# Weight splitting in a two-attention decoder layer: upper parts of w_out on ScalarE, five tiles split by halves later, a second landing place for three early weight tiles

## The reference, cut to what matters

```python
h = rmsnorm(x, norm_w[layer])
proj = h @ w_in[layer]
(sb_q, sb_k, sb_v, fx_q, fx_k, fx_v, f_logit, m_q, gate) = jnp.split(proj, offsets, axis=-1)
sb_out = stick_breaking_attention(...)   # a = beta_t * prod(1 - beta_j), strictly causal
fx_out = forgetting_attention(...)       # softmax(q.k/8 + cumulated log forget), causal
m_out = memory_attention(...)            # softmax over the 256 memory tokens
y = jnp.concatenate([merge_heads(sb_out), merge_heads(fx_out), merge_heads(m_out)], axis=-1)
yf = y.reshape(b, s, TOTAL_HEADS, HEAD_DIM)
yf = yf * lax.rsqrt(jnp.mean(yf * yf, axis=-1, keepdims=True) + EPS)
y = yf.reshape(b, s, MIX_WIDTH) * out_norm_w[layer] * jax.nn.silu(gate)
x = x + y @ w_out[layer]
return rmsnorm(x, final_norm_w)
```

## Time and profile before

| what | value |
|---|---|
| median of 3 runs | 865.62 us (864.74 to 867.26) |
| the profiled execution | 867.77 us, of which 866.0 us are the span of its instructions |
| PE busy | 817.5 us (94% of the span) |
| DVE busy | 588.7 us (68%) |
| ACT busy | 469.7 us (54%) |
| POOL busy | 278.9 us (32%) |
| mean granted TensorE clock | 0.982 |
| DMA | 88.95 MB, mean 103 GB/s |

### The profile page before, as it was taken

One profiled execution on the slowest core, in us unless ns is written; L12 is line 12 of the kernel. 1 busy time (PEld: TensorE's weight loads), 2 busy tenths in 40 slices (PEclk: granted clock), 3 DMA queues, 4 the chain that ended last, 5 costly groups with the idle time before them and its releaser, 6 DMA issues.

```text
span 866.0 us, 12221 instructions
## 1 busy us (share of the span) xinstructions
PE 817.5 (94%) x4244; PEld 682.5 (79%) x4244; DVE 588.7 (68%) x1207; ACT 469.7 (54%) x923; POOL 278.9 (32%) x387
## 2 busy tenths in 40 slices
PE   8997986899999999999999999999999997999996
PEld 7676764788888878888888888887887886878884
DVE  5745546556767787775788786778766676775575
ACT  5744555465576555667555566655555683542231
POOL 1133979423124522422353232244323111420000
PEclk9998998999999999999999999999999999999999
DMA  7013785310300320030213004030301297152432
GB/s 294 25 67 128 269 285 226 123 49 25 98 25 25 98 97 25 26 98 25 79 45 98 30 21 121 25 74 25 122 26 46 78 337 286 56 170 74 171 122 97
DMA packets 33373, 88.95 MB, mean 103 GB/s; under 512 B 3352, under 2 KB 11544, under 8 KB 32288
## 3 DMA queue, kind: packets, MB, share of 16 engines
q1 hardware_dynamic: 33312, 88.17, 30.3%
HBM read 57.72 MB, written 21.53 MB: 92 GB/s over the span
## 4 chain that ended last, share of the span: by engine, by line
PE 68%; DVE 11%; POOL 8%; ACT 5%; DMA 4%; issue 3%; SPq 0%; DVEq 0%; ACTq 0%; POOLq 0%
PE banks L682 12%; PE banks L684 11%; PE banks L683 11%; PE banks L723 9%; PE banks L823 7%; PE banks L843 4%; PE banks L842 4%; PE banks L810 3%; PE banks L809 3%; POOL w_parts L1212 3%; DVE work L1446 2%; DMA w_raw<-in_w_tiles 2%; PE banks L863 2%; DVE pT L1483 1%; DVE work L1449 1%
## 5 line engine op out<-in xcount | busy, mean ns | idle before, releaser
L682 PE MATMUL banks<-hT,w_parts 128*128 128x512 f32 x576 | 241.6, 419 | 10.2 <-DVE fx_heads L1374 3.7
L684 PE MATMUL banks<-hT,w_parts 128*128 128x512 f32 x576 | 227.1, 394 | 0.0
L683 PE MATMUL banks<-hT,w_parts 128*128 128x512 f32 x576 | 226.5, 393 | 0.0
L1483 DVE TENSOR_TENSOR pT<-banks,pT 128x512 fp32r<-128x512 f32 x208 | 112.0, 564 | 128.4 <-ACT pT L1031 127.3
L1031 ACT ACTIVATE pT<-banks 128x512 fp32r<-128x512 f32 x208 | 97.1, 498 | 178.8 <-PE banks L823 178.2
L1212 POOL TENSOR_TENSOR w_parts<-w_raw,w_parts 128x1024 fp32r<-128x1024 f32 x40 | 97.1, 2426 | 129.5 <-ACT w_parts L937 129.5
L682 PEld LDWEIGHTS banks<-hT,w_parts 128*128 128x128 f32 x576 | 109.1, 189 | 27.1 <-DVE fx_heads L1374 4.4
L684 PEld LDWEIGHTS banks<-hT,w_parts 128*128 128x128 f32 x576 | 108.7, 189 | 24.5
L683 PEld LDWEIGHTS banks<-hT,w_parts 128*128 128x128 f32 x576 | 109.4, 190 | 12.7
L1220 POOL TENSOR_SCALAR_AFFINE_SELECT work<-work 128x128 f32<-128x128 f32 x64 | 31.2, 487 | 205.0 <-ACT work L1011 205.0
L1446 DVE TENSOR_TENSOR_SCAN work<-work 128x639 f32<-128x639 f32 (+3 forms) x64 | 91.7, 1434 | 7.1 <-POOL work L1220 6.6
(11 more groups left out here) (209 smaller groups left out, 1416.7 us busy)
## 6 DMA issues: line engine op xcount, KB each, us to landing
w_raw<-in_w_tiles SPq DMA_DIRECT2D x40, 512.0 KB, 3.3
hT<-wo_dram SPq DMA_DIRECT2D x16, 512.0 KB, 8.2
work<-in_w_out SPq DMA_DIRECT2D x8, 512.0 KB, 5.9
wo_dram<-fx_heads SPq DMA_DIRECT2D x8, 512.0 KB, 4.5
wo_dram<-work SPq DMA_DIRECT2D x8, 512.0 KB, 5.3
fx_heads<-fx_heads SPq DMA_DIRECT2D x8, 512.0 KB, 7.3
negL<-negL_dram SPq DMA_DIRECT2D x8, 512.0 KB, 6.7
yT_dram<-silu SPq DMA_DIRECT2D x8, 512.0 KB, 5.2
```

Source lines behind the costliest of these rows:

```text
L682: pe.matmul(o, w[:, 0, k, :], hT[:, 0, k, tok], start=(k == 0), stop=False)
L683: pe.matmul(o, w[:, 0, k, :], hT[:, 1, k, tok], start=False, stop=False)
L684: mm = pe.matmul(o, w[:, 1, k, :], hT[:, 0, k, tok], start=False, stop=(k == KT - 1))
L1483: dve.tensor_tensor(pT[:, n % 3, 1, cols], banks[:, T_BANK + n % 2, cols], pT[:, n % 3, 0, cols].bitcast(F32), ALU.subtract).then_inc(t_lo, 1)
```

## The change

1. **Upper parts of w_out by ScalarE.** POOL's L1249 is gone; `w_out_hi` on ACT makes the upper part with an activation, POOL keeps the subtraction (`w_out_lo`).
2. **Five tiles early, five by halves later.** A tile has ten places in the order of phases. Tiles 0 to 4 are loaded at the start of phase 0 and split at ticks 4, 6, 8, 10 and 12. Tiles 5 to 9 are split as ten halves of 128x512 in phases 2 to 8: in each even phase one half in `f_row(0)` (load, split, store at ticks 1, 4, 6) and two in the first row of `negL` (ticks 8, 11, 13, and 15, 18, 20; the latter two lie in the `sb` phase behind it; phase 8 has only the first). Their loads and stores are issued by ACT, not by SP: three DMAs for each half.
3. **A second place for tiles 3, 5 and 7 of w_in.** They land in `work[:, 3S:4S]`, so that a tile can be loaded while the one ahead of it is still being split. The exponential of unit 4 waits for the splits of tile 7, since it writes there.
4. **Order in the opening.** The memory keys are copied ahead of the tile loads. ACT splits tile 6 ahead of the forget gate's exponential and logarithm.
5. **VT of phase 2** moves from ticks 27 and later to ticks 22 and 24.

```diff
-            tick = max(READ_TICK[q] + 1, UNITS * (p.of - 1) + (12 if p.of == 2 else 6))
+            tick = max(READ_TICK[q] + 1, UNITS * (p.of - 1) + 6)
...
+W_OUT_AT = [(0, 4), (2, 6), (3, 8), (4, 10), (5, 12)]
+def w_out_halves():
+    out = []
+    for ph in range(2, LAST, 2):
+        for place, load, split, store in ((0, 1, 4, 6), (1, 8, 11, 13), (1, 15, 18, 20)):
+            if place and ph == LAST - 1:
+                continue
+            j, c = len(W_OUT_AT) + len(out) // 2, len(out) % 2
+            out.append(Half(j, c, place, UNITS * ph + load, UNITS * ph + split, UNITS * ph + store))
+    return out
...
+        def w_place(n):
+            return 1 if n in (3, 5, 7) else 0
+        def w_raw_of(n):
+            return work[:, 3 * S:4 * S] if w_place(n) else w_raw[:, :]
...
             def load_tile(n):
-                sp.wait_ge(w_hi, n)
-                sp.wait_ge(w_lo, n)
-                sp.dma_start(w_raw[:, :], w_tiles[n, :, :]).then_inc(w_in_dma, 16)
+                before = [i for i in range(n) if w_place(i) == w_place(n)]
+                if before:
+                    sp.wait_ge(w_hi, before[-1] + 1)
+                    sp.wait_ge(w_lo, before[-1] + 1)
+                else:
+                    sp.wait_ge(xT_hi, KT)
+                sp.dma_start(w_raw_of(n), w_tiles[n, :, :]).then_inc(w_in_dma[w_place(n)], 16)
...
-                if closes_tile(p) and p.tile + 3 < N_TILES:
+                if p.what == "memK" and p.c == 1:
+                    copy_mem_keys(q)
+                if closes_tile(p) and p.tile < 4:
+                    load_tile(p.tile + 4)
+                if closes_tile(p) and 5 <= p.tile < N_TILES - 3:
                     load_tile(p.tile + 3)
...
+                    if u == 4:
+                        act.wait_ge(w_lo, 8)
...
+                if ph % 2 and ph < LAST:
+                    act.wait_ge(wo_half_out[0], 32 * halves_in(0, ph + 2))
+                elif 0 < ph < LAST - 1:
+                    act.wait_ge(wo_half_out[1], 32 * halves_in(1, ph + 1))
...
+            def w_out_hi(j):
+                raw, hi = wo_rows[j]
+                act.wait_ge(wo_in[j], 16)
+                act.activation(hi.bitcast(F32R), raw, ACT.Copy).then_inc(wo_hi, 1)
+            def store_w_out_half(i):
+                x = W_OUT_HALF[i]
+                raw, hi = wo_half_rows[x.place]
+                act.wait_ge(wo_lo, len(W_OUT_AT) + i + 1)
+                act.dma_start(wo_dram[x.j, 0, :, x.c * CW:(x.c + 1) * CW], hi).then_inc(wo_half_out[x.place], 16)
+                act.dma_start(wo_dram[x.j, 1, :, x.c * CW:(x.c + 1) * CW], raw).then_inc(wo_half_out[x.place], 16)
...
-                if PIECE[q].what == "F" and PIECE[q].c == 1:
+                if PIECE[q].what == "memV" and PIECE[q].c == 0:
                     act.wait_ge(f_abs, 1)
...
+                for n, x in enumerate(W_OUT_HALF):
+                    if i == x.load:
+                        load_w_out_half(n)
+                    if i == x.split:
+                        w_out_half_hi(n)
+                    if i == x.store:
+                        store_w_out_half(n)
...
-            def split_w_out(j):
-                raw, hi = wo_rows[W_OUT_LOAD[j][2]]
-                pool.wait_ge(wo_in[W_OUT_LOAD[j][2]], 16 * wo_turn(j))
-                pool.tensor_scalar(hi.bitcast(F32R), raw, 1.0, None, ALU.mult).then_inc(wo_hi, 1)
+            def w_out_lo(j):
+                raw, hi = wo_rows[j]
                 pool.wait_ge(wo_hi, j + 1)
                 pool.tensor_tensor(raw.bitcast(F32R), raw, hi, ALU.subtract).then_inc(wo_lo, 1)
```

More of the change, by code:

```diff
@@ L278 @@
 GATED_AT = [(4 * ph + 2 + i, UNITS * (ph + 1) + (END_GATE_AT if ph == LAST else GATE_AT)[i]) for ph in range(N_PH) for i in range(2)]
-W_OUT_LOAD = [(0, 3, 0), (0, 3, 1), (2, 5, 2), (3, 6, 3), (5, 8, 4), (6, 9, 5), (10, 13, 2), (12, 15, 4), (14, 17, 5), (16, 25, 3)]
-W_OUT_TURNS = [1, 1, 2, 2, 2, 2]
+Half = namedtuple("Half", "j c place load split store")
+W_OUT_AT = [(0, 4), (2, 6), (3, 8), (4, 10), (5, 12)]
[8 more added lines that the diff above has]
+    return out
+W_OUT_HALF = w_out_halves()
 RES_ORDER = [0, 1, 2, 3, 6, 4, 5]
@@ L356, in region_of, with w_loaded @@
             return sb_heads if PHASES[ph][0] == "sb" else fx_heads
+        def w_place(n):
+            return 1 if n in (3, 5, 7) else 0
+        def w_loaded(n):
+            return sum(1 for i in range(n + 1) if w_place(i) == w_place(n))
+        def w_raw_of(n):
+            return work[:, 3 * S:4 * S] if w_place(n) else w_raw[:, :]
         def v_raw(of, c):
@@ L386, in hybrid_layer, with halves_before, halves_in, wo_rows_of @@
         f_u, f_one, f_a, f_m = work[0:FH, S:2 * S], work[0:FH, 2 * S:3 * S], f_row(0)[0:FH, :], f_row(1)[0:FH, :]
-        wo_rows = [(silu[:, :], negL[:, 0, :]), (negL[:, 1, :], sb_heads[:, 7 * S:8 * S].bitcast(F32))]
-        wo_rows += [(raw, fx_heads[:, i * S:(i + 1) * S].bitcast(F32)) for raw, i in
-                    ((work[:, S:2 * S], 6), (work[:, 2 * S:3 * S], 7), (f_row(0), 0), (f_row(1), 1))]
-        def wo_turn(j):
-            return sum(1 for _, _, pair in W_OUT_LOAD[:j + 1] if pair == W_OUT_LOAD[j][2])
+        wo_rows = [(silu[:, :], negL[:, 0, :])] + [(raw, fx_heads[:, i * S:(i + 1) * S].bitcast(F32)) for raw, i in
+                                                   ((work[:, S:2 * S], 6), (work[:, 2 * S:3 * S], 7), (f_row(0), 0), (f_row(1), 1))]
+        wo_half_rows = [(row[:, 0:CW], row[:, CW:S]) for row in (f_row(0), negL[:, 0, :])]
+        def halves_before(i):
+            return sum(1 for x in W_OUT_HALF[:i] if x.place == W_OUT_HALF[i].place)
+        def halves_in(place, ph):
+            return sum(1 for x in W_OUT_HALF if x.place == place and x.load < UNITS * ph)
+        def wo_rows_of(j):
+            kind, it = PHASES[j]
+            t = it + {"sb": 0, "fx": NPAIR, "mm": 2 * NPAIR}[kind]
+            return slice(t * P, (t + 1) * P)
         free_slot = (N_TILES - 2) % 2
@@ L510, in piece_end @@
                     copy_keys(p.of, q)
-                if p.what == "memK" and p.c == 1:
-                    copy_mem_keys(q)
             def small_end(n):
@@ L595, in _ @@
             sp.dma_start(diag[:, 0, 0:KT * FH], w_forget).then_inc(wf_in, 16)
-            load_tile(1)
-            load_tile(2)
+            for n in range(1, 4):
+                load_tile(n)
             for q in range(len(FIRST)):
-                if q == len(FIRST) - 1:
-                    load_w_out(0)
-                    load_w_out(1)
                 piece_end(q)
@@ L605, in _ @@
             for i in range(X0):
-                for j, (load, split, _) in enumerate(W_OUT_LOAD):
+                for j, (load, split) in enumerate(W_OUT_AT):
+                    if i == load:
+                        load_w_out(j)
                     if i == split + 2:
                         store_w_out(j)
-                    if i == load and j > 1:
-                        load_w_out(j)
                 for q in DONE[i]:
@@ L1174, in _ @@
                     split_next(len(FIRST) - 1)
+                for j, (_, split) in enumerate(W_OUT_AT):
+                    if i == split:
+                        w_out_hi(j)
+                for n, x in enumerate(W_OUT_HALF):
[5 more added lines that the diff above has]
+                        store_w_out_half(n)
                 if i in SPREAD_AT:
@@ L1300, in _ @@
                         split_lo(PIECE[q].tile + 2)
-                for j, (_, split, _) in enumerate(W_OUT_LOAD):
+                for j, (_, split) in enumerate(W_OUT_AT):
                     if i == split:
-                        split_w_out(j)
+                        w_out_lo(j)
+                for n, x in enumerate(W_OUT_HALF):
+                    if i == x.split:
+                        w_out_half_lo(n)
         @block.vector
```

81 lines of the change are left out of this document (48 added, 33 removed).

## The result

The changed kernel takes a median of 855.0 us (853.48 to 858.0, 4 runs) where the one before takes 866.44 us (864.74 to 868.18, 4 runs): ratio 0.9872, 95% interval [0.9838, 0.9907]. In a second series on one chip it took 854.64 us (852.55 to 856.52, 4 runs) against 866.54 us (9 runs): ratio 0.9861 [0.9839, 0.9883]. The forecast was 850.1 us, its range 842 to 861: the direction and most of the gain are right, 4.9 us of the size are missing. The profiled execution took 854.92 us (span 853.2), against 852.3 forecast for it and 867.77 us before.

The account below looks back on a forecast made before the run. PE bounds phases 2 to 8; earlier, one tile buffer and POOL's w_out splits make PE idle. Gains of 19.1 less 3.6 give net 15.5 us: 867.77 to 852.3, less 2.15, a median of 850.1 us, range 842 to 861.

Parts of the forecast that it names:

- Opening, 7.4 us: Start of the kernel: with two places for tiles, PE's first filling piece starts 7.4 us sooner than at 78.57.
- The gap of 2.62 and its stretch: Phase 0: fewer POOL splits ahead of tile 8's lower part let tile 9 land in time, 4.3 us gained.
- The gap of 2.17 and its stretch: Tick 19: with POOL's list empty, two small DVE operations take 0.17 us each instead of 1.97 and more, 3.7 us gained.
- The gaps of 1.07 and 4.44: Phases 0 to 2: 2.1 of 5.5 us gained; about 3.4 us stay at tick 25, behind POOL's Newton chain.
- The gap of 1.62: Tick 22: VT no longer waits for the last store out of fx_heads, 1.6 us gained.
- Added at tick 4 and at 6 to 12: ACT waits for w_out's first tile at tick 4, 1.6 us lost; four more copies at ticks 6 to 12, 1.0 lost.
- Added in phases 2 to 8: ACT's ten copies and 30 DMA issues, and POOL's ten subtractions, cost 1.0 us in all.
- rival (d): Slower: stores issued by ACT take up to 2.13 us each, half of 42.6 us reaches PE, about 871 us; chance 0.05.
- The own range: Whole kernel: the forecast's own range for the median, from the small ends of its terms, 845 to 856 us.
- (a): Phases 0 to 2: everything comes back, copies find data landed and tick 25's gap closes, 841.4 us; chance 0.12.
- (b): Late phases: each of POOL's ten subtractions holds DVE, and DVE holds PE, 12.9 us instead of 1.0, 862.0; chance 0.14.
- (c): Phases 0 and 1: POOL was not the limit, ACT holds the same gaps, only the opening counts, 861.8 us; chance 0.07.

Follow-up runs that it names:

- experiment 5: The kernel before with only the second place for w_in tiles and the new opening order, w_out all on POOL: 858.88 us, ratio to before 0.9898.
- experiment 6: The changed kernel with POOL making the upper parts of w_out again, halves and new places kept: 851.95 us, ratio to before 0.9818.
- experiment 7: The changed kernel with two extra POOL subtractions of 128x1024 started at tick 19: 856.17 us, ratio to before 0.9876.
- experiment 8: The changed kernel with one extra POOL subtraction of 128x2048 started at tick 19: 856.06 us, ratio to before 0.9876.
- experiment 1: The changed kernel measured again with no edit: 854.64 us, ratio to before 0.9861.
- experiment 10: The changed kernel with half stores by SP, early splits later, phase 1's spread two ticks later, and upper parts by POOL: 844.91 us, ratio to before 0.9739.

## Why the prediction was right, and where its sizes were off

*Opening, 7.4 us: right.* The trace has 7.97, of which 0.78 is a difference that was there at PE's first weights matmul (18.18 before, 17.40 after), so 7.2. The last split ahead of it ends at 70.45, as the sum has it (71.2, less that 0.78). Experiment 5 measures 8.8 [7.5, 10.1] by itself, 7.3 of it up to the same place.

*The gap of 2.62 and its stretch, 4.3 us: right*, but not for ScalarE's sake: with POOL's upper parts back (experiment 6) it stays closed. There it starts at 91.70 behind four of these operations, soon enough.

*The gap of 2.17 and its stretch, 3.7 us: right, and the cause of the gap is shown.* The hold ends with POOL's operation in four traces (before, experiments 5, 7 and 8), and put back in length it brings the gap back, less the 1.8 us that are covered.

*The gaps of 1.07 and 4.44, 2.1 us.* 3.4 us of gap were to stay, 3.00 did, ended by the Newton chain (ACT waited 2.58 us for it at 135.96). What I did not see is a new gap of 1.07 at 130.63. From 125.46 to 129.27 us ACT works without a pause on VT's copy, an exponential, a table load, the gate's function and a weight split, and the transposed probabilities come behind them; it isn't there in experiment 5, where VT is not moved, but that VT's move alone makes it was not tested. So the gaps gave 1.4 us (5.5 before, 4.1 after) instead of 2.1. The slow stretch behind the 3.00 I had named and not priced. It was no gain: in 14 us from the end of the gap the clock is 0.88 before and 0.79 after, which is 1.3 us more lost in this execution, and none more in that of experiment 1 (0.88).

*The gap of 1.62, 1.6 us: right*, it is gone.

*Added at tick 4 and at 6 to 12, 1.6 and 1.0 us.* 1.51 at tick 4, as forecast and by the forecast wait (2.17 us, said 1.4 to 2.5), but only 0.58 with a wait of 1.25 us in experiment 1, so that the 1.51 agrees this well is in part luck; then 0.96 and 0.73, so 1.7 for the other term.

*Added in phases 2 to 8, 1.0 us: the term that was mis-sized.* The loss is 3.8 us: the gap of PE that ends at 218.64 us before ends 14.94 us earlier after, the one that ends at 768.32 only 11.17. Of it 3.2 are the gaps of 1.14 and 2.05. The term priced ACT's issue at 0.38 us, "since the DMA engines are busy 0.23 of these phases". Three of the twenty stores took 2.03, 1.81 and 2.71 us, the mechanism of rival (d) at about a seventh of its 21.3 us. Such a price stood in the trace of before, at these very places: SP's issue of the store of y took 2.00 us at 227.94 and 1.52 at 522.33. SP's issue of a key copy in phase 4, and the stretches of 4 us at the ticks of these three stores, in phases 2, 4 and 6:

```profile
374.25 2.64 SPq L494 DMA_DIRECT2D sb_heads<-sb_heads  x1
```
```profile
226.40:230.40 4.00, 4.00 (x21) 3.36 (x21) 1.30 (x8) 1.49 (x5) 0.48 (x2) 1.00 0.79 215
375.70:379.70 4.00, 4.00 (x25) 3.47 (x24) 2.02 (x9) 1.79 (x6) 0.59 (x2) 1.00 1.05 230
522.40:526.40 4.00, 4.00 (x24) 3.44 (x23) 2.01 (x10) 1.92 (x7) 0.59 (x2) 1.00 1.06 255
```

The mean of 0.23 hid stretches in which the DMA engines are busy nearly without a break. I should have asked for the window of each tick at which a store is issued, not for that of all phases.

*The sum.* Net 15.5 us forecast, 12.8 measured between the two spans. Against the terms the start gave 0.8 more, the opening 0.2 less, phases 0 to 2 gave 7.0 instead of 9.1, the late phases cost 2.8 more, and the end gave 1.6 more, although the change leaves it alone: in 14 us from the gap that ends at 768.32 before the clock is 0.88, and 1.00 behind the same gap at 757.15 after, which is 1.7 us. So the error of the priced terms is 5.1 us, half of it hidden by luck, the start and the end. The other 2.2 us of the miss in the median are in the step from the execution to the median: I took off 2.15 us as if the profile of after too would lie above its median, and it lies at it (854.92 and 855.0). The own range doesn't follow from its ends either: 2.1 to 5.5 and 1 to 8 give 844.1 to 854.5, not 845 to 856.

*The signs.* The first filling piece, the small DVE operation at 0.17 us and the gap at tick 25 came as said. Two signs failed: the gap of 1.07 at 130.63, and the stretch of phases 2 to 8, which is 3.8 us longer and so between the "548 to 550" of right and the "5 us or more" of wrong.

*The rivals.* (a) fell: gaps stayed at tick 25 and came at tick 4. (b) fell: ten subtractions and, in experiment 10, ten upper parts more on POOL took nothing from PE, 452.8 us between the two matmuls where it was 452.7. (c) fell: the gaps of 2.62, 2.17 and 1.62 us went with the parts of the change that spread `w_out` and move VT, and stayed in experiment 5 without them; these weren't tested one by one. (d) had the right mechanism, at 3 of its 20 stores.

*Still open.* What holds the second store. In the 2 us ahead of the three pairs of stores with a long issue the DMA share (columns of the earlier trace rows, the changed kernel) is 0.23, 1.03 and 1.04:

```profile
211.23:213.23 2.00, 2.00 (x13) 1.74 (x12) 0.80 (x4) 0.01 (x1) 2.00 (x3) 1.00 0.23 33
360.26:362.26 2.00, 2.00 (x12) 1.72 (x12) 0.88 (x4) 0.82 (x3) 0.36 (x2) 1.00 1.03 317
508.40:510.40 2.00, 2.00 (x12) 1.72 (x12) 0.88 (x4) 0.82 (x3) 0.36 (x2) 1.00 1.04 307
```

In the 4 us ahead of the seven other pairs it is 0.11 at most. So in phases 4 and 6 the long issues go with busy DMA engines, but the share doesn't decide alone: in experiment 6 it is 1.03 too ahead of phase 4's stores, and ACT's issue took 0.46 us, behind a key copy whose issue had taken SP 2.78. There SP seems to have paid in ACT's place; that was not tested. Phase 2 is another case: the engines were nearly idle, and ACT's issue (213.59 to 215.62) ran beside SP's issue of the store of y (213.45 to 215.56).

By the Trainium skill (Perfetto Trace Analysis, "DMA Instruction — HWDGE (DVE, Sync)") such an issue's time covers a wait for the shared block that makes the descriptors, and their making. In phase 2 the trace would fit such a wait, since the two issues end within 0.06 us of each other. In phase 6 it doesn't: at 510.76 the issue that SP made last had ended at 510.35.

## What to carry to other kernels

Before a DMA issue is put on a compute engine, read how long issues take in the very window where it will stand, not on average, and what the engine has behind it; the cheapest queue is one with nothing behind it. A gap costs its length and, behind the long ones in most executions here but not all, a slow stretch too, so a step that makes an engine wait for a chain is best moved to where the chain is done. And test the parts of a change alone: here the opening gave most of the gain, moving the work to other ticks removed the old gaps, and moving it to another engine gained nothing. Last, look at a second profile of the same kernel before a gap is taken for its own: here one was 1.51 us in the first and 0.58 in the next.
